# HGRN's level products on TensorE in seven visits a group, the first block of every level raised by VectorE

## What is computed

```python
b = jnp.cumsum(log_f.astype(f32).reshape(bt, nc, c, n_heads, kd), axis=2)
decay = jnp.exp(jnp.where(causal, b[:, :, :, None] - b[:, :, None, :], -jnp.inf))
attn = jnp.einsum("bcihk,bcijhk,bcjhk->bcijh", qc, decay, kc)
o_intra = jnp.einsum("bcijh,bcjhv->bcihv", attn, vc)
```

## Time and profile before

| | us |
|---|---|
| median of 3 runs (lowest, highest) | 3014.79 (3014.72, 3016.63) |
| the profiled execution | 3016.74 |
| its span | 3015.0 |
| busy: PE, DVE, ACT, POOL | 2976.6, 1751.1, 1351.2, 942.8 |
| first visit to the level products, group 0 | at 287.8 |
| last raising on POOL, last group | at 1762.3 |

### The profile page before, as it was taken

The page is one execution under the profiler, slowest core; times in us unless marked ns, Lnnn a source line. Parts: engine busy times, 40 slices in busy tenths (PEclk is TensorE's granted clock), DMA queues, the critical chain, the costliest instruction groups (busy, mean ns, idle before and its releaser), DMA issues. The chain is left out here.

```text
span 3015.0 us, 57464 instructions
## 1 busy us (share of the span) xinstructions
PE 2976.6 (99%) x22229; PEld 2828.8 (94%) x22229; DVE 1751.1 (58%) x3002; ACT 1351.2 (45%) x2650; POOL 942.8 (31%) x1086
## 2 busy tenths in 40 slices
PE   6999999999999999999999999999999999999999
PEld 5899999999999999999999999999999999998887
DVE  4746857668568476685784633344368445455554
ACT  6445456455554554555645542212243222224443
POOL 0024435246245353462353520000113343340110
PEclk9999999999999999999999999999999999999999
DMA  7723122122122221221222325442311322227653
GB/s 259 266 65 102 52 78 80 49 78 82 45 91 71 61 96 49 79 78 49 73 82 65 121 91 155 137 127 84 125 39 53 87 65 75 77 65 247 201 182 104
DMA packets 294016, 300.29 MB, mean 100 GB/s; under 512 B 13240, under 2 KB 254768, under 8 KB 293808
## 3 DMA queue, kind: packets, MB, share of 16 engines
q1 hardware_dynamic: 247968, 230.17, 24.6%
q10 hardware_dynamic: 45840, 67.27, 7.1%
HBM read 247.93 MB, written 49.46 MB: 99 GB/s over the span
## 5 line engine op out<-in xcount | busy, mean ns | idle before, releaser
L889 PE MATMUL bank<-h_hi,w_hi 128*128 128x384 f32 x2496 | 863.7, 346 | 0.0
L889 PE MATMUL bank<-h_hi,w_lo 128*128 128x384 f32 x2496 | 836.0, 335 | 0.0
L889 PE MATMUL bank<-h_lo,w_hi 128*128 128x384 f32 x2496 | 835.2, 335 | 0.0
L889 PEld LDWEIGHTS bank<-h_hi,w_hi 128*128 128x128 f32 x2496 | 469.0, 188 | 12.7 <-issue 7.3
L889 PEld LDWEIGHTS bank<-h_lo,w_hi 128*128 128x128 f32 x2496 | 469.4, 188 | 0.6
L889 PEld LDWEIGHTS bank<-h_hi,w_lo 128*128 128x128 f32 x2496 | 468.6, 188 | 0.0
L2033 POOL TENSOR_TENSOR kq<-kq,fg 128x384 f32<-128x384 f32 x288 | 291.2, 1041 | 161.3 <-PE bank L1025 130.5
L1562 DVE SCALAR_TENSOR_TENSOR acc<-bank,taps,acc 128x372 f32<-128x372 f32 (+5 forms) x512 | 249.1, 507 | 68.0 <-ACT acc L1189 56.6
L1277 ACT ACTIVATE cumb<-cumb,tok_g 128x128 f32<-128x128 f32 x576 | 176.0, 389 | 72.7 <-POOL cumb L1994 72.7
L2439 PE MATMUL bank<-a_hi,v_hi 128*128 128x384 f32 x480 | 160.9, 335 | 2.7 <-DVEq L3227 1.9
L1530 DVE TENSOR_TENSOR w_lo<-raw,w_hi 128x1024 fp32r<-128x1024 f32 x104 | 140.3, 1349 | 38.3 <-ACT w_hi L1170 38.3
(11 more groups left out here) (389 smaller groups left out, 6897.2 us busy)
## 6 DMA issues: line engine op xcount, KB each, us to landing
raw<-in_w_in SPq DMA_DIRECT2D x104, 512.0 KB, 4.1
raw<-in_ffn_w SPq DMA_DIRECT2D x78, 512.0 KB, 5.7
cumb<-cum_scratch SPq DMA_DIRECT2D x72, 512.0 KB, 6.1
ada_late<-in_ada_w SPq DMA_DIRECT2D x8, 2048.0 KB, 9.4
raw_d<-in_ffn_w SPq DMA_DIRECT2D x32, 512.0 KB, 5.4
small<-gate_scratch ACTq DMA_DIRECT2D x72, 192.0 KB, 2.4
hid_scratch<-small SPq DMA_DIRECT2D x20, 576.0 KB, 3.6
s_sum<-hid_scratch ACTq DMA_DIRECT2D x53, 192.0 KB, 3.7
```

Source lines behind the costliest of these rows:

```text
L889: last = pe.matmul(out, w[i][:, k, :], h[:, k, blk(hb)], start=(k == 0 and j == 0), stop=(k == KT - 1 and j == 2))
```

## The change

PE takes the steps of a level together. `BURSTS` gives the place of each level in eighths of a unit: levels 0 and 1 behind unit 1, level 2 in the middle of unit 3 (between its fourth and fifth depth slice), level 3 behind unit 4, level 4 in the middle of unit 6, level 5 behind unit 7, level 6 in the middle of unit 9 and level 7 behind unit 10. The transposes of v behind unit 0 stay (`turn_v`). The number of matmuls is the same.

Raising is divided. DVE raises block 0 of every level (`first_up`, in the slots of `FIRST_UP`, behind `conv_silu(k - 1)` and before `b_evac(k)`), POOL raises blocks 1 and 2. `ka` has three tiles, one for each block; the third lies in `hs_f`, which is idle then. ACT's gathers, DVE's merges and ACT's keeps are put into the slots of `KA_EARLY`, `KA_LATE`, `MERGES` and `KEEPS`; in the merges, joins and keeps themselves nothing changes.

```diff
-def steps_in(slot):
-    return [i for i in (2 * slot, 2 * slot + 1) if 0 <= i < NSTEP]
+BURSTS = {16: (0, 1), 28: (2,), 40: (3,), 52: (4,), 64: (5,), 76: (6,), 88: (7,)}
+KA_EARLY = {1: [(1, 0), (1, 1), (1, 2)], 2: [(2, 0), (2, 1)], 3: [(2, 2)], 4: [(3, 0), (3, 1)], 5: [(4, 0), (4, 1)],
+            6: [(4, 2)], 7: [(5, 0), (5, 1)]}
+KA_LATE = {4: [(3, 2)], 7: [(5, 2)]}
+FIRST_UP = {1: 1, 3: 2, 4: 3, 6: 4, 7: 5, 9: 6, 10: 7}
+MERGES = {2: (0, 1), 4: (2,), 5: (3,), 7: (4,), 8: (5,)}
+KEEPS = {10: [(6, 2)], 11: [(7, 1), (7, 2)]}
...
+        ka.append(hs_f[:, 3:6, :].rearrange("p c n -> p (c n)"))
...
+    def raised(eng, g, lv, b):
+
+        count, n = (up_first, lv) if b == 0 else (up_ready, (NB - 1) * (lv - 1) + b)
+        eng.wait_ge(count.sem, count.at(g, n))
...
                 for k in range(KT):
+                    if between is not None and k == KT // 2:
+                        levels_at(g, 8 * between + 4)
...
+            def levels_at(g, at):
+
+                for lv in BURSTS.get(at, ()):
+                    for b in range(NB):
+                        level_step(g, lv, b)
...
             def hgrn(g, k):
-                for i in steps_in(k):
...
+                levels_at(g, 8 * k + 8)
...
+            def gather_keys(g, lv, b):
+
+                if lv == 1:
+                    act.wait_ge(q_ready, g * 3 + 3)
+                else:
+                    raised(act, g, lv - 1, b)
+                s = 1 << (lv - 1)
+                act.activation(ka[b][:, :].rearrange("p (n two s) -> p n two s", two=2, s=s),
+                               pairs(0, 3, s, b * BW, BW), ACT.Copy).then_inc(ka_ready.sem, 1)
...
+            def first_up(g, k):
+
+                if k not in FIRST_UP:
+                    return
+                lv = FIRST_UP[k]
+                wait(lv_ready, g, step(lv, 0) + 1)
+                if lv == 1:
+                    dve.wait_ge(q_ready, g * 3 + 3)
+                else:
+                    raised(dve, g, lv - 1, 0)
+                if lv in (2, 3, 4, 6):
+                    wait(decay_ok, g, {2: 1, 3: 2, 4: 3, 6: 4}[lv])
+                raise_level(dve, lv, 0).then_inc(up_first.sem, 1)
...
                     if k > 0 and (k - 1) // NB in CONV_TILES:
                         conv_silu(g, k - 1)
+                    first_up(g, k)
                     b_evac(g, k)
...
-            def hgrn(g, k):
-                for i in steps_in(k):
+            def hgrn(g):
+                for lv in range(1, LEVELS + 1):
+                    for b in range(1, NB):
+                        wait(lv_ready, g, step(lv, b) + 1)
...
+                        raise_level(pool, lv, b).then_inc(up_ready.sem, 1)
```

More of the change, by code:

```diff
@@ L64 @@
 ACT_ROUND, DVE_ROUND, DT_ACT, DT_DVE = 10, 99, 6, 16
-def level(i):
-    return i // NB, i % NB
-def steps_in(slot):
-    return [i for i in (2 * slot, 2 * slot + 1) if 0 <= i < NSTEP]
+BURSTS = {16: (0, 1), 28: (2,), 40: (3,), 52: (4,), 64: (5,), 76: (6,), 88: (7,)}
[5 more added lines that the diff above has]
+KEEPS = {10: [(6, 2)], 11: [(7, 1), (7, 2)]}
 def turns_in(slot):
@@ L690, in mixers @@
     hs_loaded, decay_ok = sem("hs_loaded"), Count(sem("decay_ok"), 4)
-    up_ready = Count(sem("up_ready"), LEVELS * NB)
+    up_ready, up_first = Count(sem("up_ready"), LEVELS * (NB - 1)), Count(sem("up_first"), LEVELS)
     ka_ready = Count(sem("ka_ready"), IN_BLOCK * NB)
@@ L700, in mixers, with step, raise_level @@
     hrstd_ok, o_final, o_stored, soh_stored = sem("hrstd_ok"), sem("o_final"), sem("o_stored"), sem("soh_stored")
+    def step(lv, b):
+        return lv * NB + b
+    def raised(eng, g, lv, b):
+        count, n = (up_first, lv) if b == 0 else (up_ready, (NB - 1) * (lv - 1) + b)
+        eng.wait_ge(count.sem, count.at(g, n))
+    def raise_level(eng, lv, b):
+        s = 1 << (lv - 1)
+        n = BW // (2 * s)
+        for upper in (0, 1):
+            v = kq[:, 2 * upper:2 * upper + 2, blk(b)].rearrange(
+                "p a (n two s) -> p a n two s", two=2, s=s)[:, :, :, upper, :]
+            other = b * BW // s + 1 - upper
+            w = decays[lv - 1][:, :, other:other + 2 * n - 1:2].rearrange("p a (n s) -> p a n s", s=1)
+            ins = eng.tensor_tensor(v, v, w.broadcast_to([P, 2, n, s]), ALU.mult)
+        return ins
     def parts_at(k):
@@ L874, in _, with project @@
         def _(pe):
-            def project(g, t, b, hb, cols_n=P):
+            def project(g, t, b, hb, cols_n=P, between=None):
                 i, _, n = tile(g, t)
@@ new lines, in levels_at, with level_step @@
+            def levels_at(g, at):
+                for lv in BURSTS.get(at, ()):
+                    for b in range(NB):
+                        level_step(g, lv, b)
+            def level_step(g, lv, b):
+                i = step(lv, b)
+                if lv == 0:
+                    pe.wait_ge(q_ready, g * 3 + 1)
+                elif lv <= IN_BLOCK:
+                    pe.wait_ge(ka_ready.sem, ka_ready.at(g, i - NB + 1))
+                else:
+                    raised(pe, g, lv - 1, b)
+                if b == 0:
+                    if lv == 1 or lv == 4:
+                        pe.wait_ge(ms_read, g * NB + (2 if lv == 1 else 3))
+                    elif lv == 3 or lv == 5:
+                        pe.wait_ge(v_kept, g * NB + (2 if lv == 3 else 3))
+                    elif lv > IN_BLOCK:
+                        pe.wait_ge(lv_merged.sem, lv_merged.at(g, 1 if lv == 6 else 5))
+                for j in range(CB):
+                    c = b * CB + j
+                    s = 1 << (lv - 1) if lv else 0
+                    w = max(BS, s)
+                    for t in range(P // w):
+                        rows = slice(w * t, w * (t + 1))
+                        out = lv_out(lv, b)[rows, j * w:(j + 1) * w]
+                        own = slice(c * P + w * t, c * P + w * (t + 1))
+                        other = slice(c * P + w * (t ^ 1), c * P + w * ((t ^ 1) + 1))
+                        if lv == 0:
+                            last = pe.matmul(out, k_sum[:, own], q_t[:, own], start=True, stop=True)
+                        elif lv <= IN_BLOCK:
+                            last = pe.matmul(out.rearrange("p (n two s) -> p n two s", two=2, s=s),
+                                             ka[b][:, j * P + w * t:j * P + w * (t + 1)],
+                                             pairs(1, 2, s, c * P + w * t, w), start=True, stop=True)
+                        else:
+                            last = pe.matmul(out, (kf_t, kb_t)[t % 2][:, own], (qf_t, qb_t)[t % 2][:, other],
+                                             start=True, stop=True)
+                last.then_inc(lv_ready.sem, 1)
@@ L1034, in hgrn @@
                     if i == 0:
-                        pe.wait_ge(up_ready.sem, up_ready.at(g, LEVELS * NB))
+                        raised(pe, g, LEVELS, 0)
+                        raised(pe, g, LEVELS, NB - 1)
                     if i < 3:
@@ L1142, in _ @@
                 for k in range(SLOTS):
-                    project(g, 6 + k // NB, k % NB, b_tile(k)[1])
+                    project(g, 6 + k // NB, k % NB, b_tile(k)[1], between=k)
                     if k == 0:
@@ L1150, in _ @@
             for k in range(8 * NB):
-                project(g, 6 + k // NB, k % NB, k % NB)
+                project(g, 6 + k // NB, k % NB, k % NB, between=k)
                 if k == 0:
@@ L1300, in ssd_rstd, with hgrn_late @@
                 act.activation(rstd, rstd, ACT.Exp, scale=-0.5).then_inc(rstd_ok, 1)
+            def gather_keys(g, lv, b):
+                if lv == 1:
+                    act.wait_ge(q_ready, g * 3 + 3)
+                else:
+                    raised(act, g, lv - 1, b)
+                s = 1 << (lv - 1)
+                act.activation(ka[b][:, :].rearrange("p (n two s) -> p n two s", two=2, s=s),
+                               pairs(0, 3, s, b * BW, BW), ACT.Copy).then_inc(ka_ready.sem, 1)
+            def hgrn_late(g, k):
+                for lv, b in KA_LATE.get(k, ()):
+                    gather_keys(g, lv, b)
             def hgrn(g, k):
@@ L1308, in hgrn @@
                                       ).then_inc(hs_loaded, 16)
-                for i in steps_in(k):
[L1310 to L1325, removed]
+                for lv, b in KA_EARLY.get(k, ()):
+                    gather_keys(g, lv, b)
+                for lv, b in KEEPS.get(k, ()):
+                    wait(lv_ready, g, step(lv, b) + 1)
                     w = 1 << (lv - 1)
@@ L1457, in stage_b @@
                         conv_tanh(g, k - 1)
+                    hgrn_late(g, k)
                     if k == 12:
@@ L1689, in join_decays @@
                 if k == 4:
-                    wait(up_ready, g, NB)
+                    raised(dve, g, 1, 0)
+                    raised(dve, g, 1, NB - 1)
                 for lv in range(lo, hi):
@@ L1703, in hgrn @@
             def hgrn(g, k):
[L1704 to L1708, removed]
+                for lv in MERGES.get(k, ()):
```

(19 more changed lines are left out.)

## The result

| | before | after |
|---|---|---|
| median of 4 runs, us | 3015.71 | 3064.49 |
| lowest, highest | 3014.72, 3017.28 | 3063.57, 3065.47 |
| ratio (95% interval) | | 1.0161 (1.0148 to 1.0174) |
| the profiled execution, its span | 3016.74, 3015.0 | 3063.89, 3062.1 |
| period of the groups 0 to 6, mean | 202.4 | 209.9 |

The change makes the kernel 48.8 us slower. The periods are the distances between the first matmuls of level 0 in PE's timeline (287.8 and seven more before; 289.8, 499.2, 710.2 and so on after). Seven groups that are 7.5 us longer are 52 us. The profiled executions lie 47 us apart: the last group is 1.4 us shorter, and parts that the change leaves alone, the start and the FFN, came out 2.1 and 1.6 us shorter in this pair of executions.

A forecast was written before the change was run, and what follows sets the result against it. PE bounds stage B before; after, DVE's lag in slots 3 to 11 makes it wait. A convolution group: +8.4 + 1.6 − 1.85 = +8.2, seven +57, last group −1.4, so 3070 us; range 3000 to 3090.

The forecast's parts named there:

- What PE saves: PE's small-tile visits in stage B: grouping steps saves 1.85 us a group, 15 us in eight.
- The fixed part: PE entering and leaving the mode of small tiles: 0.33 us a visit, bounds 0.27 to 0.39.
- It doesn't group: Rival on PE's visits: a third step costs as much as a new visit, +15 us; no separate chance given.
- What DVE gets: DVE in stage B: seven pairs of raising operations a group, 1.0 us a pair, plus waits for POOL at the port.
- The ledger: DVE's time from first tap of slot 3 to last of slot 11: 50.4 us needed, against PE's 42.0.
- five pairs, with the waits in them: DVE's raising of levels 3 to 7: 5.0 us work, POOL waits of 4.3 for second operations, 2.0 for first.
- eight SiLUs waiting for POOL: DVE's L1543 in slots 3 to 11: 2.0 us of waits, half of today's 4.1.
- 8.4 us short: PE waits this long a convolution group for late banks, some 3 us each at units 6, 9 and 12.
- The ring: Join on DVE, POOL's level 4, ACT's level 5 gather and PE's burst wait in turn: 1.6 us a group, 0 to 3.
- DVE keeps up: Rival at unit 6's start: port waits under 0.3 us a group, only the saving remains, 3000 us; chance 0.20.
- Half of it: Rival: POOL lets a pair through, waits 4.5 in place of 8.7 us, 3033 (3009 to 3045); chance 0.14.
- the clock falls too: Rival: PE's pauses halve its clock, one to three falls a group, some 1.7 us each, 3082 to 3106; chance 0.11.

The follow-up runs named there:

- the pair alone: Kernel of before with its twelve visits of two steps, but DVE raises block 0 and POOL blocks 1 and 2: 3053.81 us, ratio 1.0127.
- the bursts alone: Changed kernel with its seven bursts kept, but POOL raises all three blocks and DVE none: 3038.19 us, ratio 1.0075.
- the version with pauses of up to 0.8 us (28 of them): Changed kernel, DVE's two operations take their second input from PSUM, behind the whole burst, leaving out block 0's raising: 3023.87 us, ratio 1.0029.

## Why the prediction was right

**The time.** 3070 was predicted, 3064.5 measured; slower, inside the range and inside the forecast's own 3045 to 3085.

**What PE saves.** 1.85 us a group predicted, 1.6 measured: turn_v 0.33, then 1.81, five of 0.99 and 1.40, together 8.5 in place of 8.15, against 10.1 before (slot 2's visit costs 0.84 there, and not the 0.76 that was taken). The fixed part was 0.30 and not 0.33, the step 0.23 and not 0.21 (the two came out of two rows that lie 0.21 and 0.27 apart; three kernels with one, two and three steps a visit separate them). "It doesn't group" is refuted: the third step costs 0.23.

**What DVE gets.** The ledger said 50.4 us for slots 3 to 11, the window above says 50.75. Term by term:

| us | predicted | measured |
|---|---|---|
| work without waits | 35.7 | 35.3 |
| five pairs, with the waits in them | 5.0 + 4.3 + 2.0 | 10.5 |
| eight SiLUs waiting for POOL | 2.0 | 2.0 |
| the low part of the weights (L1530, now L1565) waiting | 0.4 | 0 |
| gaps | 1.0 | 2.9 |

The work is DVE's busy 47.86 less the pairs and the SiLUs' waits. Two sizes were off, against each other: one pair of the five (337.66, 1.02 us) met nothing, since POOL had finished its four by 337.2, and DVE waits longer for ACT's tanh, 0.65 us each time that it catches up. The pattern inside a pair was other than predicted. It had one operation at 0.5 and one at 1.4 us, with 0.85 of wait for the second and 0.4 on the mean for the first; in the four pairs that met POOL both took 1.19 to 1.28, so each waits some 0.7. The sum of the two comes out near the predicted one.

**Where PE loses it.** Predicted: 8.4 us short, some 3 us each at units 6, 9 and 12; the waits of group 0 are 2.3, 2.1 and 1.6 there, and 0.2 at unit 10. Against PE's 42.0, 50.75 is 8.75 short. In group 0 it shows as 6.2 us of listed waits, as the 1.6 us that PE loses in 3.2 us at half the clock, and as what four restarts add to the listed waits, 1.0: a wait is counted from the end of the last matmul although the next would have started 0.16 us before it, and the second one follows 0.25 behind the first in place of 0.17. Together 8.8. In group 6, whose clock did not fall, the waits are 7.6 us (6.6 on the taps, 1.0 on `hs_f`).

**The ring.** 1.6 us a group taken, between 0 and 3. What shows is the wait for `hs_f`, 3.9 us in all, in four of seven groups: 0.6. This term was too large by 1.0 and, with the saving too large by 0.25, makes up for most of the difference: 8.75 + 0.6 − 1.6 = 7.75 against the period's 7.5 and the predicted 8.2. In group 0, which has no such wait, 8.75 − 1.6 = 7.15 stands against 7.1 measured (209.4 less 202.3). Waits for gathers are larger where POOL has three blocks to raise (20.7 us on `hs_f`) and where the pair stands behind the taps (also 20.7). But late taps don't start them there, so they don't show this ring; for the ring there are only the 3.9 us.

**The rivals.** *DVE keeps up* failed at its own condition, port waits under 0.3 us a group: they are 7.4 (5.4 in the pairs, 2.0 in the SiLUs). *Half of it* had waits of 4.5 us because POOL lets a pair through. They are 7.4, and the one pair in five that met nothing found POOL finished. Of *the clock falls too*, the first half came true, one fall in each of six groups. Its price did not: groups 0, 3 and 5, with a fall behind the pause at unit 6, last 209.4 us, as does group 6 without one, and groups 1, 2 and 4, with the fall behind unit 9, last 211.0, 210.5 and 210.0. PE at half speed loses 1.6 us, but DVE, which it waits for, gains them. So by this comparison, which has a single group without a fall, they cost some 3.3 us at most (1.6 + 1.1 + 0.6), where the rival had 12 to 36. The other versions bear out that it is little: with the pair behind the taps three groups with a fall last 206.7 us and three of the four without 206.3; where POOL raises all, two with a fall last 206.2 and 206.7 against 205.4, and with the copies on ACT the one group without a fall lasts 209.6 and those with one or two 208.4 to 209.3.

What stays open is why groups 1, 2 and 4 fall at the later pause, and group 6 at none. The shares of the loss were read from separate kernels and needn't add up: the pair alone costs 38 us, the bursts alone 22.5, both 48.8.

## What to carry to other kernels

Write the ledger of a stretch before giving work to an engine that is 58% busy over the span: here it was 94% busy where it mattered, and seven pairs a group of half-microsecond operations cost 38 us by themselves. When work is split between DVE and POOL, what releases both at once makes them meet; each of DVE's two operations, which read SBUF twice, then took 1.2 us in place of 0.55, about the length of one of POOL's. The same pair put behind the taps came when POOL was nearly done, and was back at 0.55 in most cases. Grouping small-tile visits is worth its fixed part (0.30 us a visit), but only as far as the engines that feed the group can deliver all of its parts together: merging two levels where DVE and POOL had room gained 4 to 5 us, and merging every level lost 22.

## What the runs showed of the hardware that had not been expected

- Of two engines that contend for the port, POOL loses too: its operations' median went from 917 ns (pair behind the taps) to 1167. Its four took 4.97 us beside DVE's three, so the two alternate and neither runs through.
- Ahead of the fall of the clock at 312.5 PE had been without a gap and then paused for 2.3 us. The length of such a pause does not decide by itself: one of 2.08 us in the same group and those of 2.27 and 2.48 us in group 6 brought no fall, while with the visits of before and DVE's pair a pause of 1.8 us stood ahead of a fall in each of seven groups, and with the pair behind the taps pauses of 1.45 and 0.43 us did in three groups of seven. In the version with pauses of up to 0.8 us (28 of them) no group had a fall. The Trainium skill (TensorE: Matmul & The Clock Gate, "HAM oscillation — how this bites in real kernels") has the idle gaps as the cause and counts half of the time at half clock as lost; that the falls come with pauses agrees, the price does not hold here, since PE waited for another engine meanwhile.
